# Modulation vectors as VectorE row sums of transposed weights, and another order of the first slab behind three norms

## What is computed

```python
c_act = jax.nn.silu(c)                       # c: (1, 2048)
mod = c_act @ w_mod[l] + b_mod[l]            # w_mod: (2048, 12288)
sh1, sc1, g1, sh2, sc2, g2 = [m[:, None, :] for m in jnp.split(mod, 6, axis=-1)]
h = rms_norm(x, norm_attn[l]) * (1.0 + sc1) + sh1
# ... h @ w_in, attention ...
x = x + g1 * mix
h = rms_norm(x, norm_ffn[l]) * (1.0 + sc2) + sh2
x = x + g2 * conv_ffn(h, w_up[l], conv_w[l], conv_b[l], w_down[l])
return rms_norm(x, norm_final)
```

## Time and profile before

| | before |
|---|---|
| median of 3 runs | 2115.6 us (2108.03, 2115.6, 2126.04) |
| profiled execution, its own time | 2109.15 us |
| its span | 2107.3 us |
| granted TensorE clock, mean | 0.99 of full |
| HBM read, written | 476.07 MB, 8.44 MB |
| DMA rate over the span | 230 GB/s |
| modulation tiles loaded | 192 of 512 KB |

### The profile page before, as it was taken

The page is one execution under the profiler, slowest core; times in us unless marked ns, Lnnn a source line. Parts: engine busy times, 40 slices in busy tenths (PEclk is TensorE's granted clock), DMA queues, the critical chain, the costliest instruction groups (busy, mean ns, idle before and its releaser), DMA issues.

```text
span 2107.3 us, 41652 instructions
## 1 busy us (share of the span) xinstructions
PE 2077.6 (99%) x17914; PEld 2047.4 (97%) x17914; DVE 1570.2 (75%) x2054; ACT 1025.7 (49%) x1331; POOL 15.4 (1%) x23
## 2 busy tenths in 40 slices
PE   7999999999999999999999999999999999999998
PEld 7999999999999999989999899999999999999998
DVE  7988688588587888697755687698765766766666
ACT  5443444344445466564457557454434444444443
POOL 1000000000000000000000000000000000000000
PEclk9999999999999999999899999999999999999999
DMA  7897898788675688578654664678866666666663
GB/s 248 279 345 277 278 320 293 239 299 321 213 266 170 203 295 276 184 257 289 213 164 116 175 183 128 204 268 287 290 185 190 190 200 192 186 204 192 197 192 121
DMA packets 248463, 480.94 MB, mean 228 GB/s; under 512 B 26315, under 2 KB 59703, under 8 KB 248279
## 3 DMA queue, kind: packets, MB, share of 16 engines
q1 hardware_dynamic: 247519, 478.06, 69.7%
q0 software_dynamic: 528, 0.15, 0.0%
q10 hardware_dynamic: 232, 0.06, 0.0%
HBM read 476.07 MB, written 8.44 MB: 230 GB/s over the span
## 4 chain that ended last, share of the span: by engine, by line
PE 94%; DVE 3%; issue 1%; DMA 1%; ACT 1%; SPq 0%; DVEq 0%; ACTq 0%
PE acc L1893 88%; PE side L1893 3%; PE sums L1893 2%; DVE mod_acc L1171 1%; PE sums L2167 1%; DMA mod_raw<-in_w_mod 1%; DVE w_lo L1183 0%; DMA x_tok<-in_x 0%; PE sums L1950 0%; DVE m_prob L1566 0%; ACT prob L1034 0%; ACT w_hi L629 0%; ACT prob L1045 0%; DVE h_lo L1591 0%; DVE kq L1543 0%
## 5 line engine op out<-in xcount | busy, mean ns | idle before, releaser
L1183 DVE TENSOR_TENSOR w_lo<-raw,w_hi 128x1024 fp32r<-128x1024 f32 x681 | 831.8, 1229 | 424.1 <-ACT w_hi L629 418.9
L629 ACT ACTIVATE w_hi<-raw 128x1024 fp32r<-128x1024 f32 x681 | 718.6, 1059 | 838.8 <-PE acc L1893 747.8
L1893 PE MATMUL acc<-h_hi,w_hi 128*128 128x256 f32 x3600 | 859.0, 280 | 11.0 <-issue 6.3
L1893 PE MATMUL acc<-h_lo,w_hi 128*128 128x256 f32 x3600 | 850.7, 278 | 0.0
L1893 PEld LDWEIGHTS acc<-h_hi,w_hi 128*128 128x128 f32 x3600 | 680.6, 189 | 22.1 <-issue 16.1
L1893 PEld LDWEIGHTS acc<-h_lo,w_hi 128*128 128x128 f32 x3600 | 680.7, 189 | 0.1
L1893 PE MATMUL acc<-h_hi,w_lo 128*128 128x256 f32 x3600 | 487.4, 278 | 0.0
L1893 PEld LDWEIGHTS acc<-h_hi,w_lo 128*128 128x128 f32 x3600 | 446.3, 189 | 0.0
L1171 DVE SCALAR_TENSOR_TENSOR mod_acc<-mod_raw,silu_c,mod_acc 128x1024 f32<-128x1024 f32 x180 | 230.4, 1280 | 11.8 <-DMA mod_raw<-in_w_mod 11.6
L1893 PE MATMUL acc<-f_hi,w_hi 128*128 128x256 f32 x704 | 164.1, 276 | 0.0
L1893 PE MATMUL acc<-f_lo,w_hi 128*128 128x256 f32 x704 | 164.0, 276 | 0.0
(11 more groups left out here) (337 smaller groups left out, 2162.2 us busy)
## 6 DMA issues: line engine op xcount, KB each, us to landing
mod_raw<-in_w_mod SPq DMA_DIRECT2D x192, 512.0 KB, 6.1
raw<-in_w_up SPq DMA_DIRECT2D x176, 512.0 KB, 4.4
raw<-in_a_w_in SPq DMA_DIRECT2D x128, 512.0 KB, 4.9
raw<-in_w_down SPq DMA_DIRECT2D x88, 512.0 KB, 4.5
raw<-in_a_w_out SPq DMA_DIRECT2D x64, 512.0 KB, 5.1
raw<-in_w_in SPq DMA_DIRECT2D x52, 512.0 KB, 3.7
raw<-in_b_w_in SPq DMA_DIRECT2D x40, 512.0 KB, 5.1
raw<-in_a_w_group SPq DMA_DIRECT2D x32, 512.0 KB, 4.8
```

The costliest lines, as they stand in the source:

```text
L629: last = act.activation(w_hi[s][:, :], raw[s][:, :], ACT.Copy)
L1183: last = dve.tensor_tensor(w_lo[s][:, :], raw[s][:, :], f32(w_hi[s][:, :]), ALU.subtract)
L1893: return pe.matmul(o, lhsT, rhs, start=start, stop=stop, skip_group_check=True)
```

## The change

The host passes `w_mod` transposed (12288x2048). A tile is now 128 outputs by 1024 inputs. `silu_c` goes; `c` is loaded as a row, broadcast to all 128 partitions (1 MB), and ScalarE makes its silu, `silu_row` of 128x2048. It takes the place of `mod_acc`, and so is loaded and made a second time ahead of the late tiles. VectorE multiplies a tile by half of `silu_row` and writes the sum of each row to one column of `mod_part`; `take_mod` adds two halves and the bias. All matmuls on modulation data go, with `mod_sum` and `mod_columns`. The late tiles start 20 slabs later and end 4 later.

The first slab behind three norms (the first block's, the second block's, the feed-forward part's) is issued in another order (`open_slab`): w_hi with h_hi, tile by tile as these are ready, then w_lo with h_hi, then w_hi with h_lo. The last product is added and squared in four tiles and not two halves, and the added squares are folded from four tiles to two on VectorE. At the start ScalarE copies the last part of x, and VectorE splits slab 0 ahead of the first `low`. The key norm's sums move into the key product, its spread ahead of the rope slab. In the last head pair `m_take_k` moves ahead of `split_to(at + 5)`. In the window attention the latent's spread moves from stage 37 to 40, and scores no longer wait for it.

```diff
-DUP_AT, IDX_PREP_AT, LAT_AT, TOP_AT = 10, 42, 34, 54
+DUP_AT, IDX_PREP_AT, LAT_AT, LAT_SPREAD_AT, TOP_AT = 10, 42, 34, 40, 54
-            (294, 128), (314, 148), (324, 148), (336, 160), (IN2_AT + 95, 160), (IN2_AT + 159, 192))
+            (294, 128), (314, 148), (324, 148), (336, 160), (IN2_AT + 115, 160), (IN2_AT + 163, 192))
...
+            def load_row():
+                sp.dma_start(silu_row[:, :], t["c_2"][0:1, :].broadcast_to([P, D])).then_inc(crow_in, 16)
...
                     if n == LATE_MODS:
                         sp.wait_ge(att[1]["mix_lo"], TILES)
+                        load_row()
...
-                    sp.dma_start(mod_raw[slot][:, :], t["w_mod_2"][0][(j // 2) * P:(j // 2 + 1) * P, bass.ds(v * D + (j % 2) * 1024, 1024)])\
+                    sp.dma_start(mod_raw[slot][:, :], t["w_mod_2"][bass.ds(v * D + (j // 2) * P, P), bass.ds((j % 2) * 1024, 1024)])\
...
                         if slabs.total() == RING:
+                            sp.wait_ge(x_squared, 4)
+                            load_row()
                             sp.dma_start(table[:, P:], ...)
...
             def square_last():
-                lasts.step()
                 act.wait_ge(sq_added, sq_adds.value(2))
-                act.wait_ge(half_added, lasts.value())
-                act.activation(tmp[1][:, 0:2, :], xT[:, 12:14, :], ACT.Square).then_inc(half_squared, 1)
+                for n in range(3):
+                    lasts.step()
+                    act.wait_ge(tile_added, lasts.value())
+                    act.activation(tmp[1][:, n, :], xT[:, 12 + n, :], ACT.Square).then_inc(tile_squared, 1)
...
+            def silu_of_row():
+                rows_silu.step()
+                act.wait_ge(crow_in, 16 * rows_silu.value())
+                act.activation(silu_row[:, :], silu_row[:, :], ACT.Silu).then_inc(csilu_ready, 1)
...
-            split(3)
+            split(1)
             for j in range(KD // 2):
                 h_part(j, by_tile=True)
-                if j == 1 or j >= 3:
-                    split(1)
+                if j == 1:
+                    act.wait_ge(x_turned, 4)
+                    act.activation(xT[:, 12:16, :], acc[1][:, :, :], ACT.Copy).then_inc(x_ready, 1)
+                split(1)
             act.wait_ge(vec_ready, 1)
-            act.activation(silu_c[:, :], vec[:, V_C:V_C + KD], ACT.Silu).then_inc(csilu_ready, 1)
+            silu_of_row()
...
-                    if j < 2:
-                        if n:
-                            dve.wait_ge(mod_summed, n // MOD_TILES)
-                        ins = dve.tensor_scalar(o, x[:, :], silu_c[:, 0:1], None, ALU.mult)
-                    else:
-                        dve.wait_ge(mod_used, n - 1)
-                        ins = dve.scalar_tensor_tensor(o, x[:, :], silu_c[:, j // 2:j // 2 + 1], o, ALU.mult, ALU.add)
+                    if j == 0:
+                        dve.wait_ge(csilu_ready, 2 if n == LATE_MODS else 1)
+                        if v >= 2:
+                            dve.wait_ge(mod_ready, v)
+                    dve.scalar_tensor_tensor(x[:, :], x[:, :], 1.0, silu_row[:, half * 1024:(half + 1) * 1024], ALU.mult, ALU.mult,
+                                             accum_out=mod_part[:, v % 2, half, c:c + 1]).then_inc(mod_used, 1)
...
             scaled(0)
-            scaled(1, (0,))
+            split(1)
             for j in range(KD // 2):
                 low(j)
                 if j == 0:
-                    scaled(1, (1,))
-                split(1)
+                    scaled(1)
+                else:
+                    split(1)
...
+                if j == 3:
+                    sq_adds.step(3)
+                    squares.step(4)
+                    keys_inverse = norm_inverse()
...
                 if last:
                     m_low(0, 2)
+                    m_take_k(n % 2)
                 split_to(at + 5)
-                m_take_k(n % 2)
+                if not last:
+                    m_take_k(n % 2)
...
+            def open_slab(a, x_hi, x_lo, tiles, hi, lo, parts):
+                openings.step()
+                pe.wait_ge(hi_ready, slabs.value(1))
+                pe.wait_ge(hi_tile_ready, openings.value())
+                for kk in range(SLAB_K):
+                    if kk == 1:
+                        pe.wait_ge(h_hi_ready, parts + 1)
+                    for i, (c0, rows) in enumerate(tiles):
+                        mm(a[0:rows, i, :], hi[:, kk, c0:c0 + rows], x_hi[:, kk, :], start=kk == 0 and i % 2 == 0)
+                pe.wait_ge(lo_ready, slabs.value(RING + 1))
+                for i, (c0, rows) in enumerate(tiles):
+                    for kk in range(SLAB_K):
+                        mm(a[0:rows, i, :], lo[:, kk, c0:c0 + rows], x_hi[:, kk, :])
...
-                    token_squares(buffers[0], range(4), True, False)
-                    lasts.step()
-                    pe.wait_ge(half_squared, lasts.value())
-                    token_squares(buffers[1], range(2), False, False)
-                    pe.wait_ge(sq_ready, squares.value())
-                    token_squares(buffers[1], range(2, 4), False, True).then_inc(sq_summed, 1)
+                    token_squares(buffers[0], range(2), True, False)
+                    last_squares(squares.value())
...
-            gemm(8, hk_hi, hk_lo, four, before=h_ready(8))
-            norm_sums([k_sq[0]], 3)
+            gemm(8, hk_hi, hk_lo, four, before=key_norm)
+            norm_spread()
             gemm(1, hk_hi, hk_lo, [(0, ROPE)], k=KD, n=ROPE)
-            norm_spread()
...
             norm_sums(tmp, 2)
-            mod_sum(norm_spread)
+            norm_spread()
...
-                    if ATT_SCORES[0][p] > LAT_AT + 3:
-                        pe.wait_ge(lat_norm, 3)
...
+    arrays["w_mod_2"] = np.ascontiguousarray(arrays["w_mod_2"][0].T)
```

178 lines of the change are left out of this document (90 added, 88 removed).

## The result

The changed kernel took 2098.9 us (median of four executions, 2083.6 to 2115.2) against 2116.1 for the kernel before (2108.0 to 2126.0). The ratio is 0.990, with a 95% interval of 0.986 to 0.994. Twelve more executions gave 0.997 (0.994 to 1.000). These ratios leave out executions over 1.5% above the lowest of their kernel, and with every execution counted nothing is left of the gain: the sixteen executions of the changed kernel have a median of 2111.3, the 122 of the kernel before that this study saw one of 2110.0. The forecast of 2073 was 26 us too low, and the time lies above its range: a gain between nothing and one per cent, where two were forecast. The four times are two near 2084 and two near 2114, so the median of 2098.9 lies between two groups, at a time that none of the sixteen executions had. The profiled execution after is one of 2112.7 us, with a span of 2110.8.

A forecast was written before the change was run, and what follows sets the result against it. TensorE, busy 2077.6 of 2107.3 us, was taken as the bound; savings of 39.1 less 1.5 for small lags gave 37.6, so 2071.5 from 2109.15, stated as 2073 with 1.5 for spread; range 2060 to 2082 (0.63), 8 in 10 2058 to 2096.

The forecast's parts named there:

- F: Key norm: squares and spread move ahead of the rope slab, so the wait for kq goes; 1.8 us gained.
- G: Last head pair: key scaling ahead of two splits removes the wait of 2.7; 0.5 us gained, at most 5.
- A: Column sums in the stream: removing their one-column matmuls from TensorE saves 20.8 us, all on the path.
- B: Second block's norm: no sums, fewer square records, earlier first slab; 6.7 us gained, 5.8 if that slab runs at low clock.
- C: Norm ahead of the feed-forward part: matmuls start 1.4 earlier, squares and folding give 1.0; together 2.5 us gained.
- E: Start: earlier norm, first matmul and second slab, less 0.9 for the long silu; net 3.0 us gained, between 1 and 4.
- H: Latent spread: last window pair's scores no longer wait 2.0 and the low clock behind goes; 3.0 us gained, at least 2.0.
- nothing takes its place on TensorE: Stream, column sums: the 20.8 us of removed sums are all on the path, with no other TensorE work replacing them.
- slabs that stay above 2.72 without any sums: Sign of being wrong: slabs slower than the plain 2.72 us although the column sums are gone.
- D: End: the same two edits in the last sum of squares, without the opening; 0.8 us gained.
- The VectorE tile: VectorE's new modulation tile with row sum: 0.1 us over the old 1280 ns, nearest to full rate; expected 1.28 to 1.45.
- The third: Rival: slabs after the sums meet transfer limits or slower VectorE; half of A, all E to H lost; 2090 to 2100; chance 0.11.

The follow-up runs named there:

- the run again: The changed kernel as it is, run again with no edit: twelve executions, ratio 0.997 (0.994 to 1.000), profiled one 2132.8 us.
- the combined kernel: The changed kernel with orders put right, plus idle one-column sets from the silu row (4, 4 and 16 columns): 2081.3 to 2084.3 us, 0.986 of the kernel before.

## Why the prediction missed

It added up 37.6 us. Without any slow stretch, and with the feed-forward's wait mended, the gain is 24.9: the execution with that edit has a span of 2082.4 against 2107.3. So 12.7 are missing from the sum: F by 7.0, G by 5.0, A by 2.8 (18.0 where I had 20.8, with set six at the net 3.4 of that execution), B by 1.2 and C by 0.1, against 1.1 more from E, 0.8 more from H and the 1.5 for small lags that need not have been subtracted. Of these 12.7 the 1.5 that I allowed for the spread must be taken off. The other 14.7, from that execution's 2084.2 to the median of 2098.9, are the pace. Its size in the median is luck, two slow executions of four; over all sixteen it is 27.

- **A, right in size but for set three.** Sets one, two and six measured 3.86, 3.83 and 3.87 (set six in the execution with a quick feed-forward part, from the slab ahead of it to the tenth behind; 0.5 of it goes to short waits elsewhere), the fourth 3.3. Set three measured 3.59 where I took 5.3. I had put 1.4 us of slower slabs behind the set down to the set. The changed kernel has no set there, and its 16 slabs of that product are slow all the same, beginning and ending with the product that reads `y_mid` (the third group's y, in another region of SBUF) and not `y`:

```profile
538.74 1.07 PE L1929 MATMUL acc<-pool_hi,w_lo 128*128 128x256 f32 x8
541.53 1.10 PE L1929 MATMUL acc<-y_mid_hi,w_lo 128*128 128x256 f32 x8
...
583.93 1.10 PE L1929 MATMUL acc<-y_mid_hi,w_lo 128*128 128x256 f32 x8
586.70 1.07 PE L1929 MATMUL acc<-y_hi,w_lo 128*128 128x256 f32 x8
```

  The two paces at one clock were there to be seen, and the step that failed here was to give them a cause within the set instead of asking what else differs.
- **The step that failed most: "nothing takes its place on TensorE", and with it the price per slab.** The sum took 2.72 us for every slab and had no term for the pace. What the runs showed in its place is a price of 2.72 or 2.83 for the same slab: 23.6 us lost over the feed-forward part of the profiled execution, and 13 of 16 executions with at least one slow stretch, against 4 of 11 without the openings. Removing the sums also removed what ended the slow pace. That the openings and the long silu add places at which it begins is likely from these counts and not shown. Why there are two paces stays open. The prediction named "slabs that stay above 2.72 without any sums" as a sign of being wrong, and it came.
- **F, wrong in sign: +1.8 forecast, -5.2 measured.** I moved the squares and the spread in thought, and did not list what stands behind the moved split on ScalarE. One more split inside the loop waits for a slab's place that TensorE frees only behind the rope slab, and two parts of h, the copy and the scaled product are queued behind it. The price is the wait of 4.6 and half a clock behind it. With the split moved back 4.8 of the 7.0 us return and a wait of 1.0 is left; the forecast gain did not come even then.
- **G, wrong in sign: +0.5 forecast, -4.5 measured.** The text said that the scaled rows come no earlier, and then priced it as a small gain. What it left out is that the wait becomes one of 4.0 in one piece, and what the clock then does. Before, waits of 2.7 and less stood there. With the order put back 4.1 of the 5.0 us return.
- **B, right in mechanism, 1.2 short of the 6.7 in the sum.** 5.5, near the 5.8 that I had given for a first slab at the low clock, and it ran at that (0.50 from 1020 to 1024, 0.71 from 1024 to 1028). VectorE's norm starts at 1018.94, the first matmul follows at 1020.11 and the second slab at 1025.37: 6.4 from the norm's first VectorE instruction, where I had 5.3 and the kernel before 10.4.
- **C, right at its slab, then spent.** 2.35 of 2.5, and 1.4 of it lost at the fifth slab, as ScalarE's splits are now what is late. "Where a stall goes, what is late next" was not asked here.
- **D, right:** 0.8. **E, better than forecast:** 4.15, the 0.9 for the long silu did not come as time. It came, in some executions, as the wait of 0.1 at 41, behind which the slow stream of 20 us begins. **H, better than forecast:** 3.8.
- **The VectorE tile, right:** 1218 ns and 82 for the sum, 0.02 over the old tile where I had taken 0.1. The rule of the Trainium skill that this form runs at half rate (Vector Engine (DVE) Microarchitecture Reference, Points that are easy to get wrong) does not hold for it here; the other one, that an accumulator output makes two instructions (VectorE: DVE Perf Modes, Two Vector instructions with no wait between them), does, as the 192 reads show.
- **The rivals.** The third, a half of A and all of E to H given back, came nearest in time (2090 to 2100) and had 0.11. Its mechanism, a VectorE that falls behind, is not what happened in the stream: VectorE's tile is as fast as the old one and the stream runs at 2.72 where it is quick. The range was too narrow, since the only term for the spread of the three executions shown (18 us) was 1.5.

## What to carry to other kernels

Look at the spread of the executions as a row of its own: 18 us in three runs of an otherwise rigid program may say that something has two values, and the trace's periods (24 matmuls in 2.72 or 2.83 at one clock) show which. For each order that is changed, write down what is queued behind the moved instruction and behind the wait that it does, on its own engine, and add what the clock costs behind a wait of TensorE of 4 us in one piece, as here. A removed instruction that stands regularly in a long stream may do more than it computes, so test its removal alone, and over ten executions.

## What the runs showed of the hardware that I had not expected

- TensorE runs 24 fp32r matmuls of 128x128 by 256 columns in 2.72 or in 2.83 us, 113 or 118 ns each, at a granted clock of 1.00 in both. The pace was kept over up to 727 us (the run again, 1383 to 2110). The changes that I looked at stood at an interruption: a wait as short as 0.08 us (1507), fp32 transposes (24.6), a norm, other operands. It goes both ways: without the feed-forward opening a matmul held up at 1527.94 was followed by the slow pace, and one at 1533.67, which took 0.32 and not 0.28, by the quick one. Not every interruption changes it: the combined kernel was held up at 1507.75 and 1513.44 and stayed quick.
- The product that reads `y_mid` was slow in every profile, quick stream or not, and so were the 19 slabs that in the kernel before run from 969 to 1023 and the 13 from 1323 to 1360. One-column fp32 products ended the slow pace when their weights lay in the row's place (sets of 16, and one of 4), and did not when they were the constant tile (sets of 16 and one of 4), though a single column of that tile was followed by the quick pace once, and four of them by the slow pace once. Why, whether by the place in SBUF, the values, the order of the output columns or something else, stays open.
- Behind waits of TensorE of 4.6 and 4.0 us the granted clock was 0.50 for some 5 us; behind one of 3.0 it was 0.59 over 4 us, behind one of 1.0 it stayed at 1.00.
- A VectorE row sum of a product of two fp32 tensors costs 1218 ns for 1024 elements and 82 for the read.
